# Gated heads of a hybrid decoder layer: the next head's diagonal products placed ahead of the samples' products

## The chip, the cores and the metric

One core of a Trainium2 chip runs the whole program. The metric is device time in microseconds (us) of one execution. All data are float32; a float32 matmul appears in the trace as two passes, so a group of 4 matmuls is listed as x8.

## The reference, cut to what matters

The layer mixes tokens by sparse attention and by gated linear attention (GLA), merges both and projects. The change lies in the GLA part, which for each of 4 heads (key width 128, value width 256) works over 1024 prompt tokens in chunks of 32 and, as a group of its own, over 8 samples of 4 tokens with a state that is loaded:

```
    b = jnp.cumsum(gc, axis=2)
    b_last = b[:, :, -1:]
    q_dec = qc * jnp.exp(b)
    k_inv = kc * jnp.exp(-b)
    k_tail = kc * jnp.exp(b_last - b)
    a_intra = jnp.where(causal, jnp.einsum('nbihd,nbjhd->nbhij', q_dec, k_inv), 0.0)
    o_intra = jnp.einsum('nbhij,nbjhv->nbihv', a_intra, vc)

    def step(S, xs):
        qd, kt, vv, bl = xs
        o_inter = jnp.einsum('bihd,bhdv->bihv', qd, S)
        S = jnp.exp(bl[:, 0])[..., None] * S + jnp.einsum('bjhd,bjhv->bhdv', kt, vv)
        return S, o_inter
```

## The kernel before, in words

The kernel is written by hand, engine by engine: each engine has one instruction stream, in order, and semaphores tie them together. No scheduler reorders anything. The GLA heads come as the last part but one; behind them stand the merging products and the output projection.

For the prompt, four chunks of 32 are handled together as a tile of 128 tokens (PT = 8 tiles, t = 0 to 7). The inputs of head h are qd and ki (decayed queries, inverse keys), kt (tail keys), Q0 and Q1 (queries decayed over one chunk and more), W4 (tail keys decayed to the tile's end) and qi. Even heads use the buffers a, odd ones b. On TensorE (PE in the trace), function `core(h)` writes one head:

- `diagonals(h, j)` for j = 0 and 1 fills PSUM bank j with the attention inside tiles 4j to 4j+3: a zero matmul (line 1337), then per tile seven small products with 32 columns of weights (lines 1326 and 1331). It needs `elem_done`, VectorE's count for Q0 and Q1 of that head. VectorE's `masked(h, j)` (line 2625) turns the bank into AT.
- `turn_tails(pe, h, j)` (line 1346) transposes W4 into banks 2 and 3, which ScalarE copies to kt (line 1525).
- `update(t)` (line 2420) is the state's addition of a tile; VectorE's `state(h, t)` (lines 2640, 2643) adds it up to S.
- for every tile the outputs: AT times values (line 2453) and qi times S (line 2457), with the turning of the next head's values (lines 1369, 1372) between them.
- the samples. First the key turns: four copies of the samples' tail keys turned (line 2473) and the samples' own attention (line 2474), both into bank 3; they count `sA_done`. VectorE's `sample(h)` makes Km and ATs of them (lines 2648, 2650) and counts `sA_ready`. Then PE does the samples' products: 16 outputs of 4 rows (lines 2483 and 2488, bank 6) and 8 state additions (line 2495, banks 3, 4, 5 and 7), counting `su_done`. VectorE's `sample_states(h)` (line 2656) waits for `su_done` and adds them to the states in 8 instructions, counting `sS_ready`.

The order around the change, at the border of head h and head h+1 (h at least 1, and not the last): key turns of h, wait for `sA_ready`, samples' products and state additions of h, diagonals of h+1, wait for all 8 `sS_ready` of h, `turn_tails` of h+1 (its banks were those of the state additions), updates of h+1.

VectorE's order there is: `sample(h)`, `tails(h+2)` (only where there is a head h+2), `tail_sums(h+1)` (W4), `sample_states(h)`, `inputs(h+1)` (qi, line 1438), `masked(h+1, 0)`, `queries(h+2)` (line 1410), `masked(h+1, 1)`, `keys(h+2)` (line 1416), `state(h+1, 0)`. In the last head the parts for h+2 are missing.

ScalarE copies outputs, squares them, and behind the samples' output makes the exponentials of h+2. In the last head it also splits the attention branch's output (`o_high`, oH, line 2889), GpSimd makes the rest of it (`o_rest`, oL, line 2594), and the first merging product on PE (line 240) waits for all four parts of oL.

SyncE starts the transfers in order; the states of the next head are loaded (line 2998) after the stores of the present one.

Of the kernel before, what the change touches and what calls it, by code (L numbers as in the profile page):

```python
# [28 lines left out]
GH, DK, DV = 4, 128, 256  # L29
# [16 lines left out]
def hybrid_step(nc, a, outs):  # L46
# [11 lines left out]
    def sem(name):  # L58
        if name not in sem_names:
            sem_names[name] = spare.pop() if spare else ctx.enter_context(  # L60
                nc.semaphore(name if stage == 0 else f"{name}_{stage}"))
        return sem_names[name]
# [22 lines left out]
    with ctx:  # L85
# [1179 lines left out]
        NV = 5  # L1265
# [52 lines left out]
        def diagonal_products(h, t):  # L1318

            i, bank, c0 = h % 2, t // 4, P * (t % 4)  # L1320
            past = (Q0[i][:, t, :], Q1[i][:, t, :], qd[i][:, P * t + 3 * CH:P * t + P])
            for x in range(4):
                rows = slice(CH * x, CH * x + CH)
                here = slice(P * t + CH * x, P * t + CH * x + CH)
                if x < 3:
                    nc.tensor.matmul(ps[rows, bank, c0 + CH * (x + 1):c0 + P], kt[i][:, here], past[x],
                                     start=False, stop=False)
            for x in range(4):
                rows = slice(CH * x, CH * x + CH)
                here = slice(P * t + CH * x, P * t + CH * x + CH)  # L1330
                mm = nc.tensor.matmul(ps[rows, bank, c0 + CH * x:c0 + CH * x + CH], ki[i][:, here], qd[i][:, here],
                                      start=False, stop=(t % 4 == 3))
            return mm

        def diagonals(h, j):

            nc.tensor.matmul(ps[:, j, :], zero[:, 0:P], zero[:, :], start=True, stop=False)
            for t in range(4 * j, 4 * j + 4):
                mm = diagonal_products(h, t)
            mm.then_inc(sem("at_done"), 1)  # L1340

        def turn_tails(pe, h, j):

            pe.wait_ge(sem("tails_ready"), h + 1)
            for t in range(4 * j, 4 * j + 4):
                mm = nc.tensor.transpose(ps[:, 2 + j, P * (t % 4):P * (t % 4) + P], W4[h % 2][:, t, :], ident[:, :])
            mm.then_inc(sem("w4_done"), 1)
# [607 lines left out]
        def _(dve):  # L1955
# [48 lines left out]
            def score(m):  # L2004
                for p in range(parts_to[m - 1] if m else 0, parts_to[m]):
                    n, _, c, w, f = parts[p]
                    r, i, br = U[n]
                    if p == 0:
                        dve.wait_ge(sem("cmp_T"), PT)
                        dve.wait_ge(sem("dist_ready"), 1)  # L2010
                    free = max(free_at[n, c + k] for k in range(w))
                    if free >= 0:
                        dve.wait_ge(sem("pT_ready"), 2 * (free + 1))
                    if n >= 8 and c == 0:
                        dve.wait_ge(sem("probs"), 2 * (n - 8) + 2)
                    nk = blocks_of[n]
                    dve.wait_ge(sem("qk_done"), m + 1)
                    b0 = SEQ if br == 1 and nk == 5 and c == 0 else SEQ - P * (nk - c)
                    for g in range(G):
                        low = mcol[:, 2 * (n % 8) + g:2 * (n % 8) + g + 1]  # L2020
                        if c > 0:
                            dve.wait_ge(sem("scored"), 2 * p + g - 1)
                        nc.vector.tensor_tensor_reduce(  # L2023
                            sP[:, g, P * (spot[n] + c):P * (spot[n] + c + w)], ps[:, g, P * f:P * (f + w)],
                            dist[:, b0:b0 + P * w], slope_of(r, g), 3e38 if c == 0 else low, ALU.add, ALU.min, low)\
                            .then_inc(sem("scored"), 1)
# [368 lines left out]
        @block.tensor  # L2395
        def _(pe):

            def core(h):
                i = h % 2
                last = h + 1 == GH  # L2400
                if h >= 1:
                    pe.wait_ge(sem("elem_done"), h + 1)
                    pe.wait_ge(sem("zl_copied"), GH)
                    for j in range(2):
                        diagonals(h, j)
                    pe.wait_ge(sem("sS_ready"), DB * h)
                    turn_tails(pe, h, 0)
                else:
                    pe.wait_ge(sem("z_out"), len(ZU))
# [62 lines left out]
                for x in range(4):  # L2472
                    nc.tensor.matmul(ps[32 * x:32 * x + ST, 3, 0:P], kt[i][:, SEQ:TOK], ident[:, :], start=True, stop=True)
                nc.tensor.matmul(ps[0:ST, 3, 2 * P:2 * P + ST], ki[i][:, SEQ:TOK], qd[i][:, SEQ:TOK],
                                 start=True, stop=True).then_inc(sem("sA_done"), 1)
                pe.wait_ge(sem("S0_loaded"), 16 * (h + 1))
                pe.wait_ge(sem("go_copied"), ncore * h + PT - 1)
                pe.wait_ge(sem("sA_ready"), h + 1)
# [20 lines left out]
            for h in range(GH):  # L2499
                core(h)  # L2500
# [627 lines left out]
```

## Time and profile before

| | |
|---|---|
| median of 3 runs | 1389.58 us (1387.01 to 1389.69) |
| the profiled execution, its own time | 1381.97 us |
| span of its profile | 1380.1 us |
| mean granted TensorE clock | 0.987 of full |
| busy: PE, VectorE (DVE), ScalarE (ACT), GpSimd (POOL) | 1307.4, 632.7, 623.8, 151.9 us |

The GLA heads take the stretch from about 1014 us to about 1113 us of the span. In the rows further down the first number is the time from the span's start, the second the duration; "PE" is the matmul, "[0.83 <-DVE ATs L2650]" means that the engine stood idle for 0.83 us before this row and that the named instruction ended the wait. PEclk 1.00 is 2.4 GHz, 0.50 is 1.2 GHz.

### The profile page before, as it was taken

The page shows a single profiled execution, that of the slowest core. Times are in us where ns is not written, and L with a number is a line of the kernel's source. Part 1 is how long each engine was busy: PE and PEld are TensorE (multiplying, and loading weights), DVE is VectorE, ACT ScalarE, POOL GpSimd, SP SyncE. Part 2 cuts the span into 40 slices and gives each one's busy share as a digit, 9 for nine tenths or more (in the row PEclk, how much of TensorE's full clock was granted, in tenths as well). Part 3 has the DMA queues.
Part 4 walks back from the last instruction along what each step waited for, and adds up shares of the span by engine and source line. Part 5 has one row for each costly group of instructions (what it writes and reads, how often), then busy time and mean ns, then how long its engine had stood idle before and what let it go on. Part 6 is the DMA issues. An engine that isn't in the chain of part 4 may idle for free.

```text
span 1380.1 us, 23623 instructions
## 1 busy us (share of the span) xinstructions
PE 1307.4 (95%) x9533; PEld 1174.8 (85%) x9533; DVE 632.7 (46%) x1395; ACT 623.8 (45%) x1072; POOL 151.9 (11%) x185
## 2 busy tenths in 40 slices
PE   5999998998999999999999999999988988999998
PEld 5999998998978888988988889788865678999876
DVE  6211145644834343433233332467588766453342
ACT  6212236542465546555456545665476542221121
POOL 2100001103300000100000300313010270000000
PEclk9999999999999999999999999999998999999999
DMA  7251453422321211222212212545254746542231
GB/s 203 65 169 35 140 122 103 144 67 55 83 63 52 69 47 58 63 75 67 63 57 78 63 57 68 177 150 149 87 192 149 238 152 191 159 134 84 96 126 61
DMA packets 156908, 145.27 MB, mean 105 GB/s; under 512 B 27360, under 2 KB 141360, under 8 KB 156736
## 3 DMA queue, kind: packets, MB, share of 16 engines
q1 hardware_dynamic: 154016, 135.33, 32.5%
q0 software_dynamic: 2784, 8.43, 2.1%
q8 instruction: 76, 1.25, 0.4%
q14 instruction: 32, 0.26, 0.1%
HBM read 105.88 MB, written 41.88 MB: 107 GB/s over the span
## 4 chain that ended last, share of the span: by engine, by line
PE 65%; DVE 5%; ACT 2%; issue 2%; POOL 1%; DMA 0%; POOLq 0%; DVEq 0%; another core or an unknown queue 0%; SPq 0%; ACTq 0%
PE ps L240 38%; PE ps L2545 6%; PE ps L1671 5%; PE ps L1705 4%; PE ps L1687 4%; PE ps L1720 1%; POOL oL L2594 1%; DVE S L2656 1%; PE ps L1790 1%; PE ps L2553 1%; PE ps L1641 0%; PE ps L2512 0%; PE ps L1744 0%; PE ps L1624 0%; ACT sP L2262 0%
## 5 line engine op out<-in xcount | busy, mean ns | idle before, releaser
L240 PE MATMUL ps<-hH,wH 128*128 128x352 f32 (+1 forms) x1320 | 441.0, 334 | 11.5 <-ACT stg L360 6.0
L240 PE MATMUL ps<-hH,wL 128*128 128x352 f32 (+1 forms) x1320 | 426.1, 323 | 0.0
L240 PE MATMUL ps<-hL,wH 128*128 128x352 f32 (+1 forms) x1320 | 425.8, 323 | 0.0
L240 PEld LDWEIGHTS ps<-hH,wH 128*128 128x128 f32 (+1 forms) x1320 | 248.9, 189 | 38.5 <-issue 26.9
L240 PEld LDWEIGHTS ps<-hL,wH 128*128 128x128 f32 (+1 forms) x1320 | 249.9, 189 | 2.2 <-issue 1.9
L240 PEld LDWEIGHTS ps<-hH,wL 128*128 128x128 f32 (+1 forms) x1320 | 248.7, 188 | 0.3
L227 DVE TENSOR_TENSOR wL<-w_raw,wH 128x1024 fp32r<-128x1024 f32 (+1 forms) x70 | 85.7, 1225 | 135.3 <-ACT wH L219 135.2
L2023 DVE CUSTOM_DVE_ANT_0 sP<-ps,dist,stat 128x256 f32<-128x256 f32 (+3 forms) x116 | 58.5, 542 | 181.8 <-issue 104.4
L360 ACT ACTIVATE stg<-ps 128x352 f32<-128x352 f32 x132 | 61.0, 462 | 116.4 <-PE ps L240 107.6
L219 ACT ACTIVATE wH<-w_raw 128x1024 fp32r<-128x1024 f32 (+1 forms) x70 | 73.5, 1049 | 70.8 <-issue 39.5
L2219 ACT ACTIVATE pPT<-ps 128x512 f32<-128x512 f32 x74 | 44.0, 595 | 134.7 <-PE ps L1687 134.7
L2262 ACT ACTIVATE sP<-sP,stat 128x640 f32<-128x640 f32 (+7 forms) x128 | 93.0, 728 | 13.4 <-DVE stat L2023 11.7
L2023 DVE CUSTOM_DVE_ANT_0 sP<-ps,dist 128x128 f32<-128x128 f32 (+3 forms) x128 | 46.5, 408 | 93.6 <-PE ps L1671 93.6
L1671 PE MATMUL ps<-kT,qT 64*128 64x256 f32 (+3 forms) x440 | 75.8, 455 | 3.4 <-DVE stat L2023 3.4
L1705 PE MATMUL ps<-pPT,vtok 128*64 128x128 f32 x1056 | 72.8, 279 | 1.4 <-issue 1.4
L1881 POOL TENSOR_TENSOR tmp<-tmp 128x256 f32<-128x256 f32 x16 | 16.5, 1033 | 484.4 <-DVE tmp L2058 484.4
L1687 PE MATMUL ps<-ident,sP 128*128 128x128 f32 x528 | 69.2, 273 | 0.5 <-ACT sP L2262 0.4
L1705 PEld LDWEIGHTS ps<-pPT,vtok 128*64 128x64 f32 x1056 | 56.5, 136 | 12.9 <-issue 12.6
L240 PE MATMUL ps<-ogH,m_wH 128*128 128x352 f32 x192 | 62.3, 324 | 2.7 <-DVE ogL L2767 2.7
L1687 PEld LDWEIGHTS ps<-ident,sP 128*128 128x128 f32 x528 | 60.9, 140 | 3.3 <-ACT sP L2262 1.3
L240 PE MATMUL ps<-ogH,m_wL 128*128 128x352 f32 x192 | 62.9, 328 | 0.0
L240 PE MATMUL ps<-ogL,m_wH 128*128 128x352 f32 x192 | 62.7, 326 | 0.0
(395 smaller groups left out, 2069.8 us busy)
## 6 DMA issues: line engine op xcount, KB each, us to landing
w_raw<-in_w_in SPq DMA_DIRECT2D x61, 512.0 KB, 4.1
p_spill<-stg SPq DMA_DIRECT2D x132, 176.0 KB, 1.8
zt<-p_spill SPq DMA_DIRECT2D x24, 528.0 KB, 4.8
w_raw<-in_w_in SPq DMA_DIRECT2D x17, 256.0 KB, 3.8
gvT<-p_spill SPq DMA_DIRECT2D x8, 528.0 KB, 5.6
x_all<-in_x_prompt SPq DMA_DIRECT2D x8, 512.0 KB, 9.2
m_raw<-in_w_branch_b SPq DMA_DIRECT2D x8, 512.0 KB, 5.4
xr<-in_x_prompt SPq DMA_DIRECT2D x8, 512.0 KB, 3.5
```

Of the source, the lines that this page charges most:

```text
L219: nc.scalar.activation(self.wH[:, c % 2, 0:n], self.raw[:, c % self.nraw, 0:n], ACT.Copy)\
L227: nc.vector.tensor_tensor(self.wL[:, c % 2, 0:n], self.raw[:, c % self.nraw, 0:n], self.wH[:, c % 2, 0:n].bitcast(F32), ALU.subtract).then ...
L240: mm = nc.tensor.matmul(ps[0:t.m, bank, 0:NF], w[:, c % 2, t.m * k:t.m * k + t.m], x[n][:, k, :], start=(k == 0 and i == 0), stop=(k == t. ...
L360: nc.scalar.activation(stg[:, u % NSTG, :], ps[:, bank, 0:NF], func, scale=DK ** -0.5 if t.kind == "gq" else 1.0).then_inc(sem("f_act"), 1)
L1671: mm = nc.tensor.matmul(ps[:, g, P * f:P * (f + w)], qT[rows, r, P * i:P * i + P], kT[rows, br, P * k0:P * (k0 + w)], start=True, stop=True)
L1687: mm = nc.tensor.transpose(ps[:, 4 + g, P * (f + k):P * (f + k) + P], sP[:, g, P * b:P * b + P], ident[:, :])
L1705: mm = nc.tensor.matmul(ps[HD * g:HD * g + HD, 6 + j % 2, col:col + P], vtok[:, key, P * br + HD * g:P * br + HD * g + HD], pPT[:, m % NPT ...
L1881: link(nc.gpsimd.tensor_tensor(t[:, 0:2 * P], t[:, 0:2 * P], t[:, 2 * P:4 * P], ALU.add))
L2023: nc.vector.tensor_tensor_reduce(sP[:, g, P * (spot[n] + c):P * (spot[n] + c + w)], ps[:, g, P * f:P * (f + w)], dist[:, b0:b0 + P * w], s ...
L2219: copy = lambda dst, src: nc.scalar.activation(dst, src, ACT.Copy)
L2262: nc.scalar.activation(p, p, ACT.Exp, bias=mcol[:, 2 * (n % 8) + g:2 * (n % 8) + g + 1], scale=-1.0, accum_out=lcol[:, j % 2, g, br, i % 2 ...
L2545: mm = nc.tensor.matmul(ps[0:n, bank, :], m, w[half][:, k, :], start=(k == 0 and i == 0), stop=(k == KT - 1 and i == 2))
```

## The change: what it does

The wait and the two halves of the diagonals become a function, `next_diagonals(h)`. Head 1 calls it at its start as before. For heads 2 and 3 it is called by the head before, right behind the samples' key turns and ahead of the waits for the samples' products. A wait for the values' copies of head h-1 and h is added (`gv_copied`), since these used banks 0 and 1 last; `core` had it later anyway.

```
+            def next_diagonals(h):
+
+                pe.wait_ge(sem("elem_done"), h + 1)
+                pe.wait_ge(sem("zl_copied"), GH)
+                pe.wait_ge(sem("gv_copied"), NV * (h + 1))
+                for j in range(2):
+                    diagonals(h, j)
+
             def core(h):
                 i = h % 2
                 last = h + 1 == GH
                 if h >= 1:
-                    pe.wait_ge(sem("elem_done"), h + 1)
-                    pe.wait_ge(sem("zl_copied"), GH)
-                    for j in range(2):
-                        diagonals(h, j)
+                    if h == 1:
+                        next_diagonals(h)
                     pe.wait_ge(sem("sS_ready"), DB * h)
                     turn_tails(pe, h, 0)
...
                 nc.tensor.matmul(ps[0:ST, 3, 2 * P:2 * P + ST], ki[i][:, SEQ:TOK], qd[i][:, SEQ:TOK],
                                  start=True, stop=True).then_inc(sem("sA_done"), 1)
+                if h >= 1 and not last:
+                    next_diagonals(h + 1)
                 pe.wait_ge(sem("S0_loaded"), 16 * (h + 1))
                 pe.wait_ge(sem("go_copied"), ncore * h + PT - 1)
                 pe.wait_ge(sem("sA_ready"), h + 1)
```

PE's instructions at the border of head 1 and head 2 before. ATs, Km and S_3300 are the samples' masked attention, turned keys and states; zero opens a bank of the diagonals, Q0a to ki_3278 are inputs of head 2's diagonals, W4a its tail keys:

```order
L2474 MATMUL ps<-qd_3279,ki_3283 32x32
L2483 MATMUL ps<-S_3300,qd_3279 4x256 x4
L2488 MATMUL ps<-vh_3293,ATs 4x256 x4
...
L2495 MATMUL ps<-vh_3293,Km 128x256 x8
L1337 MATMUL ps<-zero 128x512
L1326 MATMUL ps<-Q0a,kt_3280 32x96
L1326 MATMUL ps<-Q1a,kt_3280 32x64
L1326 MATMUL ps<-qd_3278,kt_3280 32x32
L1331 MATMUL ps<-qd_3278,ki_3282 32x32 x4
...
L1346 MATMUL ps<-ident,W4a 128x128 x8
```

The same place with the change (its lines are numbered 6 to 8 higher from `core` on):

```order
L2480 MATMUL ps<-qd_3279,ki_3283 32x32
L1337 MATMUL ps<-zero 128x512
L1326 MATMUL ps<-Q0a,kt_3280 32x96
L1326 MATMUL ps<-Q1a,kt_3280 32x64
L1326 MATMUL ps<-qd_3278,kt_3280 32x32
L1331 MATMUL ps<-qd_3278,ki_3282 32x32 x4
...
L2491 MATMUL ps<-S_3300,qd_3279 4x256 x4
L2496 MATMUL ps<-vh_3293,ATs 4x256 x4
...
L2503 MATMUL ps<-vh_3293,Km 128x256 x8
L1346 MATMUL ps<-ident,W4a 128x128 x8
```

The diagonals of head 2 (two zero matmuls and 56 small ones) moved from behind the state additions to ahead of the samples' products. Now nothing stands between the state additions and the tail keys' turns. The border of head 2 and head 3 has changed in the same way, with the buffers a and b exchanged.

VectorE's instructions there, the same in both kernels but for line numbers (these are of the change):

```order
L2656 TENSOR_TENSOR Km<-ps,bmt 128x256
L2658 TENSOR_TENSOR ATs<-ps,tris 32x32
...
L1438 TENSOR_TENSOR W4a<-kt_3280,dec_3276 128x1024
L2664 SCALAR_TENSOR_TENSOR S_3300<-S_3300,ebs_3266,ps 128x256 x8
L1438 TENSOR_TENSOR qi_3284<-qd_3278,dec_3276 128x1024
L2633 TENSOR_TENSOR AT<-ps,tri 128x512
```

Nothing moved here: the eight state updates stand ahead of qi and of the masking (AT) that reads the diagonals.

## Rows read from the trace of the kernel before

**Rows 1.** The page's list of engines: busy us, share, instructions.

```profile
PE 1307.4 (95%) x9533; PEld 1174.8 (85%) x9533; DVE 632.7 (46%) x1395; ACT 623.8 (45%) x1072; POOL 151.9 (11%) x185
```

**Rows 2.** Timeline of PE, end of head 1, start of head 2.

```profile
1065.54 0.23 PE L2474 MATMUL ps<-qd,ki 128*32 128x32 f32 x2
1066.59 0.61 PE L2483 MATMUL ps<-S,qd 128*4 128x256 f32 x8 [0.83 <-DVE ATs L2650]
...
1068.76 1.15 PE L2495 MATMUL ps<-vh,Km 32*128 32x256 f32 x16
1069.84 0.50 PE L1337 MATMUL ps<-zero 128*128 128x512 f32 x1
...
1072.54 0.28 PE L1331 MATMUL ps<-qd,ki 128*32 128x32 f32 x3
1073.25 1.09 PE L1346 MATMUL ps<-ident,W4a 128*128 128x128 f32 x8 [0.42 <-DVE S L2656]
...
1078.72 0.70 PE L2457 MATMUL ps<-S,qi 128*128 128x256 f32 x2 [0.77 <-DVE S L2643]
```

**Rows 3.** Timeline of VectorE, the same place.

```profile
1069.97 3.22 DVE L2656 SCALAR_TENSOR_TENSOR S<-S,ebs,ps 128x256 f32<-128x256 f32 x8 [1.04 <-PE ps L2495]
1073.11 1.22 DVE L1438 TENSOR_TENSOR qi<-qd,dec 128x1024 f32<-128x1024 f32 x1
1074.25 0.68 DVE L2625 TENSOR_TENSOR AT<-ps,tri 128x512 f32<-128x512 f32 x1
...
1078.24 0.42 DVE L2643 COPY S<-ps 128x256 f32<-128x256 f32 x1
```

**Rows 4.** Timeline of PE, end of head 2, start of head 3.

```profile
1088.58 0.23 PE L2474 MATMUL ps<-qd,ki 128*32 128x32 f32 x2
1089.64 0.61 PE L2483 MATMUL ps<-S,qd 128*4 128x256 f32 x8 [0.83 <-DVE ATs L2650]
...
1092.88 0.50 PE L1337 MATMUL ps<-zero 128*128 128x512 f32 x1
...
1095.59 0.28 PE L1331 MATMUL ps<-qd,ki 128*32 128x32 f32 x3
1096.30 1.09 PE L1346 MATMUL ps<-ident,W4b 128*128 128x128 f32 x8 [0.42 <-DVE S L2656]
```

**Rows 5.** Timeline of VectorE, the same place.

```profile
1093.02 3.22 DVE L2656 SCALAR_TENSOR_TENSOR S<-S,ebs,ps 128x256 f32<-128x256 f32 x8 [2.40 <-PE ps L2495]
```

**Rows 6.** The chain that ended last, from head 3 on: start, us, what.

```profile
1104.45 1.08 ACT oH L2889
1105.61 10.50 POOL oL L2594 x4
...
1183.25 94.36 PE ps L240 x576
```

**Rows 7.** Timeline of PE: three waits, around 1034, 1116 and 1142 us.

```profile
1034.65 0.70 PE L2453 MATMUL ps<-vh,AT 128*128 128x256 f32 x2 [2.22 <-ACT og L2875]
...
1116.15 0.66 PE L240 MATMUL ps<-oH,m_wH 128*128 128x352 f32 x1 [3.15 <-POOL oL L2594]
...
1142.97 0.22 PE L2512 MATMUL ps<-ident,og 32*128 32x32 f32 x1 [3.02 <-DVE zt L2762]
```

**Rows 8.** Stretches of 1 us: length, busy us by engine, PEclk, DMA, GB/s.

```profile
1036.00:1037.00 1.00, 1.00 (x12) 0.56 (x10) 1.00 (x2) 0.74 (x3) 0.00 (x0) 0.50 0.49 143
1114.00:1115.00 1.00, 0.00 (x0) 0.00 (x0) 1.00 (x4) 0.94 (x5) 1.00 (x1) 0.73 0.02 5
1121.00:1122.00 1.00, 1.00 (x7) 1.00 (x7) 0.00 (x0) 0.00 (x0) 1.00 (x1) 0.86 1.10 382
1143.00:1144.00 1.00, 1.00 (x6) 0.96 (x7) 0.52 (x2) 0.45 (x1) 0.00 (x0) 1.00 0.00 0
```

**Rows 9.** SyncE's queue, the load of head 2's states, and its time.

```profile
1079.22 0.38 SPq L2998 DMA_DIRECT2D S<-in_state_gla x1
DMA to landing us min/median/max: 5.3/5.3/5.3
```

## The prediction

> **What bounds the kernel now.** I read the page first: PE is busy for 95% of the span [rows 1], so at first sight anything that fills a hole of PE is a gain. Then the timelines of the place that changes, of PE and of VectorE side by side, to see which wait ends last there. At the border of head 1 and head 2, PE finishes the key turns at 1065.77 (1065.54 + 0.23), stands until VectorE has made Km and ATs, and begins the samples' products at 1066.59 [rows 2]: a hole of 0.82 us. The state additions follow, and with their end VectorE begins its 8 state updates at 1069.97, after standing idle for 1.04 us [rows 3]. So VectorE waits for PE here. While VectorE updates (3.22 us), PE does the diagonals, from 1069.84 to 1072.82 (2.98 us), then waits 0.42 us for the updates' end before it may turn the tail keys [rows 2]. The reader is to see two things: the diagonals stand today under VectorE's updates, where PE has nothing else it may do, and the updates are on the path. Behind them VectorE works without a gap through qi, the masking and the next head's queries and keys to the first state at 1078.24 [rows 3], and PE's output product waits 0.77 us for that one [rows 2]. The border of head 2 and 3 has the same shape: a hole from 1088.81 to 1089.64 (0.83 us), diagonals from 1092.88 to 1095.87 (2.99 us), PE waiting 0.42 us for VectorE [rows 4], VectorE idle for 2.40 us ahead of its updates [rows 5]. There the turned tail keys are what PE needs next.
>
> **The change, part by part.** No instruction that computes is added or removed; two blocks of diagonals move, once for head 2 and once for head 3. Head 0 to 1 stays as it was, so nothing differs before 1065.77.
>
> *What the move fills.* The diagonals need Q0 and Q1 of the next head, made long before, so they can start at once. They fill 0.82 and 0.83 us of hole. The added wait for the values' copies costs nothing: these were copied in the middle of the head; if they were not, the old kernel would wait for them a little later.
>
> *What the move delays.* 2.98 us of diagonals go into a hole of 0.82 us, so the samples' products, the state additions and with them VectorE's updates begin 2.98 - 0.82 = 2.16 us later; at the second border 2.99 - 0.83 = 2.16 us. VectorE cannot take it up, being idle already (1.04 and 2.40 us); its idle time merely grows to 3.2 and 4.6 us.
>
> *What leaves the path.* Nothing. The place that the diagonals leave was covered by the updates: without them PE waits not 0.42 us but some 3.4. In short, the path before is hole + samples + max(diagonals, updates), after it is max(diagonals, hole) + samples + updates; the difference is min(diagonals, updates) - hole = 2.98 - 0.82. That the diagonals are done earlier helps no one: VectorE reaches the first masking at 1074.25, at its own pace, 1.4 us after they ended [rows 2, 3].
>
> *Who else waits.* Behind the diagonals on PE stand only the samples' products. ScalarE's copy of the samples' output, its exponentials and SyncE's transfers shift by the same 2.16 us as VectorE, so no new wait among them. The load of head 2's states starts at 1079.22 and took 5.3 us [rows 9], needed at 1089.64 [rows 4]: 5.1 us to spare, and both shift. At the end of the heads the chain goes from oH on ScalarE through four rests on GpSimd (10.50 us) to the first merging product at 1116.15 [rows 6, 7], later through unbroken stretches of PE such as 94.36 us [rows 6]. That oH stands in ScalarE's stream behind an output of head 3, so it moves with the heads. I find nothing behind it that is set by a clock of its own. Sum of the two borders: 4.32 us.
>
> *The clock.* PE will now stand idle from the end of the state additions to the end of the updates: 3.22 us plus the 0.1 or so of hand-over, 3.3 us, at each border. Rows for waits of this size point both ways. A wait of 2.22 us ended at 1034.65, and by 1036 the granted clock was 0.50, that is 1.2 GHz. One of 3.15 us ended at 1116.15; the clock fell to it within 1114, during the wait, and was back at 2.4 GHz within 1121. One of 3.02 us ended at 1142.97, and the clock behind it was 1.00 [rows 7, 8]. Two of three fell. The price of one fall, estimated from the stretch of 7 us that began in idleness: some 5 us of it lie on work, which then moves at half speed and loses 2.5 us. At the start of head 2 PE has 0.77 us of waiting to give [rows 2], so about 1.7 us remain; at the start of head 3, 2.5 us. Bounds: nothing at all, and for both borders with a fall that lies on work for its whole 7 us, 3.5 - 0.8 + 3.5 = 6.2 us. I take one fall of the two, at their mean, 2.1 us. With two falls in three waits, one to two are to be expected; I lean to one, since the waits nearest in length to the new ones (3.15 and 3.02 us) went once each way.
>
> The Trainium skill, "TensorE: Matmul & The Clock Gate", section "HAM oscillation — how this bites in real kernels", says that a wait between two bursts of matmuls lets the gate throttle and that every next burst then starts at half rate. By that rule both borders would pay, which is the second rival below; the wait that ended at 1142.97 speaks against "every" [rows 7, 8].
>
> Sum: 4.32 + 2.1 = 6.4 us more than the kernel before. Against the profiled execution (1381.97) that is 1388.4; against the median of the runs (1389.58), which lies 7.6 us above the profiled one for reasons that this trace doesn't show, 1396.0 us. I forecast runs, so the latter.
>
> **The rivals.**
>
> *The clock never falls at the borders* (chance 0.27): 4.3 us, 1393.9. For it speaks the wait that ended at 1142.97.
>
> *The clock falls at both* (0.20): 4.3 us of delay, 1.7 us at head 2 and 2.5 us at head 3, 8.5 us together, 1398.1. For it, two falls of three in this trace.
>
> *The delay is taken up later* (0.12): one or both shifts of 2.16 us never reach the end, because something unshifted sets the start of the merging products or of a later weight tile. The time is 1389.6 to 1391.7. Against it: the chain runs unbroken from head 3 through oH and oL into PE.
>
> *Faster, since the hole is larger than what is put into it* (0.04). By the two paths above the change can win only where the diagonals take longer than the updates, and then from a hole of 3.2 us, the length of the updates, on; at most it wins what sticks out of the updates. That is so at a low clock, where the diagonals take twice 2.98, 6.0 us: 2.8 us stick out, and with a hole of 6 us all of it is won, 1386.8. The hole would come from the states' load, which is waited for at the same place. But it would have to come over 10 us later at the second border (5.1 us to spare and 5 more), and nothing in the rows shows that.
>
> That the change doesn't do what it says is excluded by the order of the instructions.
>
> **How the numbers follow.** Forecast (one fall's worth, +6.4) 0.37, no fall 0.27, both fall 0.20, taken up 0.12, faster 0.04. About 0.2% (2.8 us) is what a measurement of this kernel can tell from no change. The first three cases lie above it: 0.84, less a little for the scatter of three runs (2.7 us): 0.83 slower. The taken-up case is mostly within: 0.13. Faster 0.04. The range runs from one shift alone (1391.7, rounded down to 1391.5) to 4.3 + 6.2 = 10.5 us (1400.1, taken as 1400.0); what it leaves out is part of the taken-up case and the faster one.
>
> **What would show it.** Right: in the new profile L2483's counterpart starts about 3.0 us after the key turns' end at both borders with its wait gone; VectorE's idle time before the state updates is about 3.2 and 4.6 us; PE waits about 3.4 us before L1346, put down to the updates; the first masking still doesn't wait for PE; oH begins 4.3 us later or more, and PEclk shows 0.50 in at least one head's start. Wrong: an idle time before the updates that hasn't grown; a first merging product still at 1116; a head 2 or 3 that starts its outputs sooner than before.

## The result, and the profile after

| | before | changed |
|---|---|---|
| median of 20 runs each | 1386.66 us | 1393.28 us |
| lowest and highest | 1383.36, 1389.69 | 1388.60, 1396.90 |
| ratio of the times, 95% interval | | 1.0043 [1.0034, 1.0052] |
| profiled execution, span | 1381.97, 1380.1 us | 1396.90, 1395.0 us |

The change makes the kernel 0.43% slower by the ratio, 6.0 us on 1386.66, with an interval from 4.7 to 7.2 us; the two medians are 6.6 us apart. The two profiled executions are 14.9 us apart, and that is no measure of the change: head 1's key turns end at 1065.77 before and at 1073.84 after, 8.1 us apart at a point which the change hasn't yet touched. So I read two stretches. The **first stretch** goes from the end of head 1's key turns to the end of head 2's and holds the first border; the **second stretch** goes from there to the first oH and holds the other.

| stretch | before | changed |
|---|---|---|
| first | 1065.77 to 1088.81, 23.04 us | 1073.84 to 1099.86, 26.02 us |
| second | 1088.81 to 1104.45, 15.64 us | 1099.86 to 1118.58, 18.72 us |

Together 38.68 us became 44.74 us: 6.06 us, which lies within the measured loss. The far ends of the second stretch and of what follows it, in the changed kernel:

```profile
1118.58 1.07 ACT L2897 ACTIVATE oH<-oF 128x1056 fp32r<-128x1056 f32 x1
1130.27 0.66 PE L240 MATMUL ps<-oH,m_wH 128*128 128x352 f32 x1 [3.15 <-POOL oL L2602]
```

From the first oH to the first merging product it is 11.70 us before and 11.69 us here, and from there to the end of the span 264.0 and 264.7 us. So nothing is taken up behind the borders.

The timeline of PE in the changed kernel, the two borders (compare [rows 2, 4]; the lines' numbers are 6 to 8 higher):

```profile
1073.61 0.23 PE L2480 MATMUL ps<-qd,ki 128*32 128x32 f32 x2
...
1076.53 0.39 PE L2491 MATMUL ps<-S,qd 128*4 128x256 f32 x3
...
1078.73 1.15 PE L2503 MATMUL ps<-vh,Km 32*128 32x256 f32 x16
1083.23 1.97 PE L1346 MATMUL ps<-ident,W4a 128*128 128x128 f32 x8 [3.35 <-DVE S L2664]
1085.12 2.90 PE L2426 MATMUL ps<-vh,kt 128*128 128x256 f32 x6
...
1099.63 0.23 PE L2480 MATMUL ps<-qd,ki 128*32 128x32 f32 x2
...
1104.77 1.15 PE L2503 MATMUL ps<-vh,Km 32*128 32x256 f32 x16
1109.26 1.97 PE L1346 MATMUL ps<-ident,W4b 128*128 128x128 f32 x8 [3.35 <-DVE S L2664]
1111.15 2.12 PE L2426 MATMUL ps<-vh,kt 128*128 128x256 f32 x6
1113.32 0.43 PE L2447 MATMUL ps<-ident,oN 32*128 32x32 f32 x4
```

The hole ahead of the samples' products (L2491) is gone, but they now begin 2.69 us behind the key turns' end instead of 0.82. And the wait ahead of the tail keys' turns (L1346) has grown from 0.42 to 3.35 us. The turns themselves take 1.97 us instead of 1.09, at the low clock (the stretches of 1 us further down).

The timeline of VectorE there (compare [rows 3, 5]):

```profile
1079.95 3.22 DVE L2664 SCALAR_TENSOR_TENSOR S<-S,ebs,ps 128x256 f32<-128x256 f32 x8 [2.94 <-PE ps L2503]
1083.09 1.22 DVE L1438 TENSOR_TENSOR qi<-qd,dec 128x1024 f32<-128x1024 f32 x1
1084.22 0.68 DVE L2633 TENSOR_TENSOR AT<-ps,tri 128x512 f32<-128x512 f32 x1
...
1105.98 3.22 DVE L2664 SCALAR_TENSOR_TENSOR S<-S,ebs,ps 128x256 f32<-128x256 f32 x8 [4.31 <-PE ps L2503]
1109.12 2.95 DVE L1438 TENSOR_TENSOR qi<-qd,dec 128x1024 f32<-128x1024 f32 x1
```

The state updates begin 6.11 and 6.12 us behind the key turns' end; it was 4.20 and 4.21 us (1069.97 and 1093.02). That is 1.91 us of delay at each border, and VectorE's idle time ahead of them grew by the same 1.9 us. The masking still follows qi without waiting for PE.

The granted clock, in stretches of 1 us (columns as in [rows 8]):

```profile
1081.00:1082.00 1.00, 0.00 (x0) 0.00 (x0) 1.00 (x4) 1.00 (x2) 0.00 (x0) 0.81 0.02 5
1085.00:1086.00 1.00, 1.00 (x3) 0.82 (x3) 1.00 (x1) 0.60 (x1) 0.00 (x0) 0.50 0.54 177
1088.00:1089.00 1.00, 1.00 (x5) 0.79 (x4) 0.77 (x3) 0.23 (x1) 0.00 (x0) 0.77 0.63 208
1108.00:1109.00 1.00, 0.00 (x0) 0.00 (x0) 1.00 (x4) 0.00 (x0) 1.00 (x2) 0.97 0.03 8
1112.00:1113.00 1.00, 1.00 (x5) 0.73 (x4) 1.00 (x3) 0.00 (x0) 1.00 (x1) 0.82 0.82 229
```

At both borders the clock fell to 1.2 GHz while PE waited. By the shares in these rows it came back 6.8 us later at the first (it fell within 1081 and rose within 1088) and 3.4 us later at the second (within 1108, within 1112).

### The profile page after: what moved, and what is told of

Read it like the earlier page. It is cut to its first block, busy times and chain, and to the rows that moved or that the text cites. A ratio compares the mean times of both kernels' runs of the same rounds, so it can differ in the third digit from the quotient of the medians.

```text
span 1395.0 us, 23623 instructions
## 1 busy us (share of the span) xinstructions
PE 1319.2 (95%) x9533; PEld 1185.6 (85%) x9533; DVE 633.2 (45%) x1395; ACT 623.7 (45%) x1072; POOL 151.6 (11%) x185
## 4 chain that ended last, share of the span: by engine, by line
PE 66%; DVE 5%; ACT 2%; issue 2%; POOL 1%; DMA 0%; POOLq 0%; DVEq 0%; another core or an unknown queue 0%; SPq 0%; ACTq 0%
PE ps L240 38%; PE ps L2553 6%; PE ps L1671 5%; PE ps L1705 4%; PE ps L1687 4%; PE ps L1720 1%; POOL oL L2602 1%; DVE S L2664 1%; PE ps L1790 1%; PE ps L2561 1%; PE ps L1641 0%; PE ps L2426 0%; PE ps L2459 0%; PE ps L2520 0%; PE ps L1624 0%
```

## The experiments

Ten runs: eight kernels of mine, one of them twice, and the changed one again. All stretches in one table; "fell" says whether PEclk stood at 0.50 behind the wait of that border.

| run | first, us | second, us | sum | clock at the two borders | ratio to before, 95% |
|---|---|---|---|---|---|
| before | 23.04 | 15.64 | 38.68 | up, up | |
| changed | 26.02 | 18.72 | 44.74 | fell, fell | 1.0043 [1.0034, 1.0052] |
| changed, again | 25.15 | 19.84 | 44.99 | fell, fell | 1.0024 [1.0011, 1.0037] |
| diagonals twice | 24.93 | 17.86 | 42.79 | up, up | 1.0041 [1.0025, 1.0056] |
| half of them moved | 23.66 | 17.32 | 40.98 | fell, fell | 1.0014 [1.0004, 1.0024] |
| first border only | 26.10 | 15.87 | 41.97 | fell, up | 1.0037 [1.0023, 1.0052] |
| second border only | 23.04 | 19.93 | 42.97 | up, fell | 1.0028 [1.0016, 1.0041] |
| changed, qi early | 26.07 | 18.61 | 44.68 | fell, fell | 1.0039 [1.0024, 1.0055] |
| changed, masks early | 24.57 | 17.88 | 42.45 | fell, fell | 1.0033 [1.0017, 1.0048] |
| before, qi early | 22.03 | 15.66 | 37.69 | up, up | 0.9989 [0.9978, 1.0000] |
| before, qi and turns early | 21.93 | 15.14 | 37.07 | up, up | 0.9983 [0.9971, 0.9995] |
| the same, again | 21.92 | 15.16 | 37.08 | up, up | 0.9997 [0.9983, 1.0011] |

The stretches repeat within 0.1 us where the clock and the length of qi are the same (the second stretch is 0.23 us longer in one run whose qi was 0.33 us longer); the times of whole executions carry an interval of 1 to 2 us to each side. So mechanisms are read from the stretches, and the times only bound them. In one run they disagree: the profile of the changed kernel's repetition shows 6.3 us on the two stretches, which is 0.46%, while its times say 0.24% with an upper end of 0.37%. The size of the loss is therefore less certain than the stretches alone would make it.

**The diagonals twice: the delay without the wait.** `next_diagonals` runs in the changed place without counting, and again in the old place, counting `at_done`.

```
-                    if h == 1:
-                        next_diagonals(h)
+                    next_diagonals(h)
...
-                    next_diagonals(h + 1)
+                    next_diagonals(h + 1, False)
```

> The diagonals of heads 2 and 3 are computed twice: once in the changed place (not counted) and once in the old place behind the state additions (counted), so the output is whole. Theory (delay through the state updates, plus a clock that falls in the wait which the move leaves behind): the delay alone remains, since PE has work under the updates again; the stretch from the end of head 1's key turns to the first oH, 38.7 us before and 44.7 us after, takes 38.7 + 4.3 = 43.0 us, the clock does not fall at the two borders, the time is +4.3 us (+0.3%) on the kernel before. Rival (the clock has no part, the move costs 6 us by itself): 44.7 us as in the changed kernel. Rival (PE's own work is the bound): 6.0 us of added diagonals less 1.7 us of hole, also +4.3, but then PE's wait ahead of the tail keys' turns is gone; under the theory it is still about 0.4 us.

Measured: 42.79 us, the clock up at both borders. PE in this run, around the second set and the turns:

```profile
1077.22 1.09 PE L1347 MATMUL ps<-ident,W4a 128*128 128x128 f32 x8 [0.43 <-DVE S L2664]
...
1105.37 0.43 PE L2447 MATMUL ps<-ident,oN 32*128 32x32 f32 x4 [0.23 <-DVE AT L2633]
```

PE still waits 0.43 us for the updates, as before, although it does 3 us more per border than the kernel before: the diagonals are covered in the old place, and all that they add in the new one is delay. The first stretch is 1.89 us longer than before, equal to the updates' delay. The second is 2.22 us longer: 1.91 of delay, and PE then waits 0.23 us for the masking, because qi took 2.08 us here instead of 1.67. That is 4.1 us for both, the delay of 3.8 and the longer qi, where 4.3 were expected. With PE's wait covered, 2.0 of the changed kernel's 6.06 us are gone, so they come with the wait that the move leaves behind. The rival by which the move alone costs 6 us falls. The times of this run and of the changed kernel can't be told apart (1.0041 and 1.0043 or 1.0024), so the split rests on the stretches alone.

**Half of them moved.**

`next_diagonals` is told which of the two banks it has to fill.

```
-                    if h == 1:
-                        next_diagonals(h)
+                    next_diagonals(h, (0, 1) if h == 1 else (1,))
...
-                    next_diagonals(h + 1)
+                    next_diagonals(h + 1, (0,))
```

> Only the first bank of the diagonals (1.45 us) goes ahead of the samples' products, the second stays behind the state additions. Theory: each border pays 1.46 - 0.82 = 0.64 us, VectorE's idle time ahead of its updates is 1.7 and 3.0 us, the stretch from head 1's key turns to the first oH is 38.7 + 1.3 = 40.0 us if the clock stays up (PE idles 1.8 us per border), total +0.1%. Rival (the cost lies in the place of the diagonals as such, in proportion to what is moved): half of 6 us, 41.7 us.

Measured: 40.98 us. The updates' delay is 0.45 us (4.65 us behind the key turns at each border), less than the 0.64 expected. But PE now waited 1.89 us, and the clock fell at both borders all the same:

```profile
1074.65 1.97 PE L1346 MATMUL ps<-ident,W4a 128*128 128x128 f32 x8 [1.89 <-DVE S L2663]
...
1098.31 1.79 PE L1346 MATMUL ps<-ident,W4b 128*128 128x128 f32 x8 [1.89 <-DVE S L2663]
```

The first stretch grew by 0.62 us, the second by 1.68 us, of which 1.2 are not delay. The fall at the second border began 0.2 us after the wait had ended. The rival's 41.7 us is nearer to 40.98 than my 40.0, which left the fall out; the parts, 0.45 us of delay against 1.91, speak against anything in proportion.

**One border at a time.**

```
-                if h >= 1 and not last:
+                if h + 1 == 2:
```

and the same with 3; the other head's diagonals stay in the old place.

> Only head 2's diagonals move (border of head 1 and 2), head 3's stay. Theory: the stretch from the end of head 1's key turns to the end of head 2's is 26.0 us with a fall of the clock (23.04 before, 26.02 after), 25.2 without; the rest up to the first oH stays at 15.6 us. Total +2.2 to +3.0 us. Rival (a delay at one border is absorbed and only both together show): no change, 38.7 us for the whole stretch.

> Only head 3's diagonals move (border of head 2 and 3). Theory: up to the end of head 2's key turns nothing changes (23.0 us), from there to the first oH 18.7 us (15.64 before, 18.72 after): 2.2 us of delay and some 0.9 us from VectorE's qi, which took 2.95 us beside GpSimd instead of 1.67 us, and from the low clock. Total +3 us. Since GpSimd's gating here starts at another distance from qi than in the changed kernel, qi may be shorter or longer: this run shows whether the 0.9 us follow qi's length or PEclk.

Measured: 26.10 and 15.87 us with the first border alone, 23.04 and 19.93 us with the second alone. The untouched border costs nothing, so the two add up and nothing is absorbed. (The 0.23 us in 15.87 go with a qi of 2.00 us, behind which PE waits 0.15 us for the masking.) The second border alone cost 4.3 us, not 3, with these rows:

```profile
1104.68 1.97 PE L1346 MATMUL ps<-ident,W4b 128*128 128x128 f32 x8 [3.35 <-DVE S L2664]
...
1106.58 2.90 PE L2426 MATMUL ps<-vh,kt 128*128 128x256 f32 x6
...
1108.66 0.48 DVE L2648 SCALAR_TENSOR_TENSOR S<-S,dec,ps 128x256 f32<-128x256 f32 x1 [0.29 <-PE ps L2426]
```

Here qi took 2.29 us, less than the 2.95 of the changed kernel, and the stretch is longer by 1.2 us all the same: VectorE waits for PE's state products. The clock was low for 6.8 us:

```profile
1103.00:1104.00 1.00, 0.00 (x0) 0.00 (x0) 1.00 (x4) 0.00 (x0) 1.00 (x2) 0.93 0.01 4
1109.00:1110.00 1.00, 1.00 (x7) 0.53 (x5) 0.23 (x2) 0.00 (x0) 0.05 (x1) 0.50 1.08 385
1110.00:1111.00 1.00, 1.00 (x4) 0.88 (x4) 0.48 (x4) 0.00 (x0) 0.00 (x0) 0.66 1.03 300
```

**Is it qi's length or the clock?** The changed kernel with VectorE's `inputs(h + 1)` ahead of `sample_states(h)`:

```
-                sample_states(h)
                 if next1:
                     inputs(h + 1)
+                sample_states(h)
```

> The changed kernel, with VectorE's qi of the next head ahead of its state updates (borders 1 to 2 and 2 to 3), where it now idles for 2.9 and 4.3 us. The updates' start stays 6.1 us behind the key turns' end. Theory: at the border of head 2 and 3, qi runs before GpSimd's gating has begun or in its first microseconds and takes 1.2 to 2 us instead of 2.95, and the masking starts right behind the updates; PE then goes on at the pace of its own clock. The stretch from head 2's key turns to the first oH, 18.7 us in the changed kernel, is 17.6 us without a fall of the clock and 18 to 20 with one (19.9 was seen where the clock was low for 7 us). At the border of head 1 and 2, PE rather than VectorE sets the outputs' start after a fall: 26.0 us stays within 0.3; without a fall 24.2. Rival (qi's length never set anything): no change of either stretch for the same clock.

Measured: qi takes 1.21 us and stands in VectorE's idle time, and the second stretch is 18.61 us against 18.72. The clock fell within 1097 and was back within 1100, for about as long on work as in the changed kernel. The first stretch, 26.07 us against 26.02, hasn't changed either. This is the rival of the expectation: at the low clock qi's 2.95 us set at most 0.1 us, and the excess over the delay is the clock's. With the delay alone the second stretch would be 15.64 + 1.91 = 17.55 us; it was 18.6 to 18.7 us where the clock was low for 3.4 us, and 19.8 to 19.9 us where it was low for 6.8 us.

**The changed kernel once more.**

> The changed kernel once more, for a second profile and for times beside the other two. Theory: the updates start 6.1 us behind the key turns' end at both borders again, whatever the clock; both stretches lie between 24.9 and 26.1 us and between 17.6 and 20 us, by when the clock falls and comes back; +0.3 to +0.5% on the kernel before.

Measured: 25.15 and 19.84 us, both clocks fell, after the same waits of 3.35 us:

```profile
1073.94 1.76 PE L1346 MATMUL ps<-ident,W4a 128*128 128x128 f32 x8 [3.35 <-DVE S L2664]
...
1099.09 1.97 PE L1346 MATMUL ps<-ident,W4b 128*128 128x128 f32 x8 [3.35 <-DVE S L2664]
```

At the first border the clock fell only as PE's work began and was back within 1077, which cost 0.2 us beside the delay; at the second it was low from within 1098 to within 1104, which cost 2.3 us. The sum is nearly that of the first profile by chance. Its ratio of 1.0024 is lower than the first measurement's and than the 0.3% expected at least; the upper end of its interval, 1.0037, lies within the other's.

**Could the early diagonals be used?** In heads 1 and 2 VectorE does qi and both maskings of the next head ahead of its updates, and the first tail keys' turns come ahead of PE's wait:

```
+                    turn_tails(pe, h, 0)
                     pe.wait_ge(sem("sS_ready"), DB * h)
-                    turn_tails(pe, h, 0)
...
-                masked(h, 0)
+                if h == 1:
+                    masked(h, 0)
...
-                sample_states(h)
                 if next1:
                     inputs(h + 1)
+                    masked(h + 1, 0)
+                    masked(h + 1, 1)
+                sample_states(h)
```

`masked(h, 1)` gets the same condition, and ScalarE's copy of the first turns moves ahead of its last exponential, as shown for the next kernel.

> The changed order of PE, used by VectorE: in heads 1 and 2 qi and both maskings of the next head stand ahead of the state updates, in the time in which VectorE idles, and the first tail keys' turns come ahead of the wait as in the run before. Theory: the updates still begin 1.9 us later than in the kernel before, but 2.4 us of VectorE's work has left the path behind them, so each border comes out about as before the change: 23.0 and 15.6 us without a fall of the clock, 1 to 2 us more with one; that is 3 to 6 us faster than the changed kernel, within 0.2% of the one before. Rival (the early diagonals do win once VectorE uses them): below 22.5 and 15.0 us.

Measured: 24.57 and 17.88 us. Against the changed kernel that wins 2.3 us, where 3 to 6 were expected, but it stays 3.8 us behind the kernel before, and its time is 0.33% above it, not within 0.2%. PE waits 2.76 us for the updates, and the clock falls at both borders:

```profile
1098.75 1.12 PE L1346 MATMUL ps<-ident,W4b 128*128 128x128 f32 x4 [2.76 <-DVE S L2664]
```

The rival (below 22.5 and 15.0) falls. The next kernel makes the same moves of qi and of the turns with the diagonals in the old place, and its two stretches sum to 37.07 us against 42.45 here. So in this version the early diagonals don't pay although they are used. What it would do with the clock up was not measured; 38.6 us were expected.

**What can be moved instead.** In the kernel before, qi goes ahead of the updates at all three borders, the first four turns go ahead of PE's wait, and ScalarE's copy of them ahead of its last exponential:

```
+                    turn_tails(pe, h, 0)
                     pe.wait_ge(sem("sS_ready"), DB * h)
-                    turn_tails(pe, h, 0)
...
                         exps(act, h + 1)
+                    tail_keys(act, h, 0)
+                    if next1:
                         tail_exps(act, h + 1)
-                    tail_keys(act, h, 0)
```

> The kernel before, with its diagonals in the old place, and the holes used otherwise: qi ahead of the state updates at all three borders (VectorE idles 3.7, 1.0 and 2.4 us there), the first four tail keys' turns (bank 2, which the state additions don't use) ahead of PE's wait for the updates, and ScalarE's copy of them ahead of its last exponential. Theory (what is worth moving is what stands behind the updates on the path, not what they cover): border 0 to 1 about 1.1 us shorter (28.7 to 27.5), border 1 to 2 about 1.0 us (23.0 to 22.0), head 2's key turns to the first oH about 1.2 us (15.6 to 14.4), together 3.3 us, 0.24% faster than before. Rival (the borders are bound elsewhere): no change.

> The kernel before with qi alone ahead of the state updates, at all three borders; PE and ScalarE as before. It separates the two edits of the run with both (21.9 us from head 1's key turns to head 2's, 15.1 us from there to the first oH; 23.0 and 15.6 before). If qi did it: the first stretch is 22.3 us (PE then waits less than before for the first state), the second 15.6, since there PE waits for the turned keys. If the tail keys' turns did it: 23.0 and 15.1. The time is 0 to 0.15% below the kernel before.

> The run with qi and the first tail keys' turns moved, once more, beside the changed kernel on one chip. 0.1 to 0.25% faster than the kernel before again, 0.5 to 0.6% faster than the changed one; if its first measurement was luck, no difference.

Measured: both edits give 21.93 and 15.14 us, and 21.92 and 15.16 in the repetition; qi alone gives 22.03 and 15.66. So qi is worth 1.0 us in the first stretch (0.7 were expected of qi alone), the turns 0.5 us in the second (1.2 were expected there of both edits: in the repetition the diagonals end 0.4 us ahead of the updates' end, so there is hardly time left for turns under the updates). At the border of head 0 and 1 the clock was low for different lengths. Four profiles are alike there, low once for 6.8 us from 3.4 to 3.7 us behind head 0's key turns. From these to head 1's key turns it takes 28.14 and 28.27 us where qi is in its old place (the changed kernel's repetition, and the run with the masks early), 27.24 us with qi early and 27.58 us with both edits: 0.6 to 1.0 us less, where 1.1 were expected. By time this version was 0.17% faster than before in one measurement, with an interval that excludes 1, and 0.03% in the other, with one that doesn't; the 1.6 us that the stretches show (0.12%) lie in both. Measured beside it, the changed kernel's repetition has a median of 1385.94 us against 1381.23: 0.3% more, where 0.5 to 0.6% were expected. Beside the kernel before, I call the gain shown in the stretches, not settled in the time.

```profile
1067.08 1.22 DVE L1438 TENSOR_TENSOR qi<-qd,dec 128x1024 f32<-128x1024 f32 x1
1068.22 3.21 DVE L2656 SCALAR_TENSOR_TENSOR S<-S,ebs,ps 128x256 f32<-128x256 f32 x8
1071.35 0.68 DVE L2625 TENSOR_TENSOR AT<-ps,tri 128x512 f32<-128x512 f32 x1
```

These rows of the repetition show what is different from [rows 3]: qi stands where VectorE idled for 1.04 us, and the masking follows the updates directly.

## Why the prediction was right

- **The direction and the mechanism.** Right. The state updates are on the path, the diagonals were covered by them, and moving the diagonals out delays the updates. Nearly all the markers came out: idle times of 2.94 and 4.31 us (forecast 3.2 and 4.6), a wait of 3.35 us ahead of L1346 (3.4), no wait at the masking, oH later by the full amount, PEclk at 0.50 in the starts of both heads. Only the samples' products start 2.7 us behind the key turns, not 3.0.
- **The time.** 1396.0 us were forecast and 1393.28 measured. The difference is in the starting point: the median of three runs before the change, 1389.58 us, became 1386.66 us over twenty. The added time was forecast as 6.4 us and came out as 6.0 us by the ratio, 6.6 us by the medians. That it came so close is in part luck: the delay was 0.5 us too large, and one fall at too high a price stood for two cheap ones.
- **The delay term.** Mis-sized: 2.16 us per border forecast, 1.91 us measured, 3.8 instead of 4.3 us for both. The step was "2.98 us of diagonals go into a hole of 0.82 us". The 2.98 us run from the block's first start to its last end, and blocks overlap at both seams: in the changed kernel the diagonals start at 1073.76, 0.08 us ahead of the key turns' end, and the samples' products start 0.2 us ahead of the diagonals' end. So the products start 2.69 us behind the key turns, not 2.98.
- **The clock term.** 2.1 us forecast, 2.2 us measured (6.06 - 3.82), 2.5 in the second profile, 2.0 by comparison with the run that covers the wait. The size was right, the way to it was not: I took one fall at 1.7 or 2.5 us. Both borders fell in both profiles, and a fall cost 0.2 to 1.2 us at the first border and 1.1 to 2.4 us at the second, by how much of the low stretch lies on work. The rival with two falls had the right count and too high a price. The rule of the Trainium skill ("TensorE: Matmul & The Clock Gate", section "HAM oscillation — how this bites in real kernels"), which I held to be too strict, held at these borders: the clock was at 1.2 GHz by the end of each of the waits of 1.89, 2.76 and 3.35 us or within 0.3 us of it, twelve waits in seven profiles. It did not hold everywhere. The wait of 3.02 us in [rows 7] is one exception, and head 0 has more. There the same wait of 2.22 us stands in all twelve profiles. In six the clock fell within 1.5 us behind it, in the other six it stayed up through this wait and the next one, of 2.41 us, and fell only 1.0 to 2.1 us behind that. The changed kernel's two profiles, the first with a fall within 1044, the repetition without one until 1040:

```profile
1042.73 0.70 PE L2459 MATMUL ps<-vh,AT 128*128 128x256 f32 x2 [2.22 <-ACT og L2883]
1044.00:1045.00 1.00, 1.00 (x13) 0.61 (x11) 1.00 (x2) 0.81 (x4) 0.00 (x0) 0.54 0.32 70
...
1034.38 0.70 PE L2459 MATMUL ps<-vh,AT 128*128 128x256 f32 x2 [2.22 <-ACT og L2883]
1038.81 0.61 PE L2491 MATMUL ps<-S,qd 128*4 128x256 f32 x8 [2.41 <-DVE ATs L2658]
1039.00:1040.00 1.00, 1.00 (x20) 0.21 (x16) 0.97 (x3) 0.31 (x1) 0.00 (x0) 1.00 0.00 0
1040.00:1041.00 1.00, 1.00 (x12) 0.11 (x9) 1.00 (x2) 0.00 (x0) 0.00 (x0) 0.53 0.00 0
```

Ahead of the waits at the two borders PE always did the samples' small products; whether the wait alone would bring the clock down was not separated.
- **Who else waits.** Right that nothing is absorbed: the borders add up, and the way from oH to the first merging product is the same to 0.01 us.
- **A cause that I had not named.** GpSimd's gating lengthened VectorE's qi to 2.95 us. With the low clock it set at most 0.1 us, by the run with qi early. With the clock up a qi of 2.00 or 2.08 us went with 0.23 us.

## What to carry to other kernels

Before filling a hole of the busiest engine, ask what covers the work where it stands now: here the diagonals cost nothing under the state updates, and moving them cost the lesser of both lengths less the hole. Leaving PE nothing to do in a wait can have a second price: at these two borders, after standing still for 1.9 to 3.4 us, it went on at half clock and paid 0.2 to 2.4 us more.

## What the runs showed of the hardware that I had not expected

- PE's clock fell during or within 0.3 us of waits as short as 1.89 us at these two borders, and stayed up at both in every run with a wait of 0.4 us. Elsewhere waits of 2.22, 2.41 and 3.02 us passed without it. A low stretch at these borders lasted 3.4 or 6.8 us, in either order in the two profiles of one program.
- VectorE's multiplication for qi, 1.22 us elsewhere and 1.21 us ahead of GpSimd's gating, took 1.52 to 2.95 us while GpSimd multiplied; the state updates and the maskings, which read PSUM, kept their 3.22 and 1.27 us for two beside it. In all seven profiles where the two met, qi ended 1.12 or 1.13 us after GpSimd's next multiplication had begun, and that one took 3.3 us instead of 2.35. In the kernel before, 0.55 us of GpSimd's running multiplication were left when qi started (1096.16, the next at 1096.71), in the changed one 1.83 us (1109.12, 1110.95); that is the whole difference between 1.67 and 2.95 us.
- The profiled span up to a point that two programs have in common differed by 8.1 us. Two spans of this kernel say little about a change of 6 us.
